# Two gate tiles of each merge step computed from seven block products instead of eight in chunks 1 to 3

## The reference

```python
h = rmsnorm(x, norm_g)
proj = h @ w_in                     # 1024 x 9216; the last 3072 columns are the gates
y_a = (conv module, width 31) @ w_a_out
y_b = (differential attention, 4 heads) @ w_b_out
y_c = (short gated convolution, width 3) @ w_c_out
g = sigmoid(gates + gate_b).reshape(b, s, 3, 1024)
merged = g[:, :, 0] * y_a + g[:, :, 1] * y_b + g[:, :, 2] * y_c
out = rmsnorm(x + merged @ w_o, final_g)
```

## Time and profile before

| | |
|---|---|
| median of 3 runs | 2287.43 us (2286.47 to 2288.08) |
| the profiled execution | 2287.08 us, its span 2285.3 us |
| TensorE busy | 2258.3 us, 99% of the span |
| VectorE, ScalarE, GpSimd busy | 62%, 33%, 10% |
| granted TensorE clock | 0.999 of the full 2.4 GHz |
| the three merge stages of chunks 1 to 3 | 133.6, 133.6 and 134.0 us |
| DMA | 493.53 MB, mean 216 GB/s |

### The profile page before, as it was taken

One profiled execution on the slowest core, in us unless ns is written; L12 is line 12 of the kernel. 1 busy time (PEld: TensorE's weight loads), 2 busy tenths in 40 slices (PEclk: granted clock), 3 DMA queues, 4 the chain that ended last, 5 costly groups with the idle time before them and its releaser, 6 DMA issues.

```text
span 2285.3 us, 29046 instructions
## 1 busy us (share of the span) xinstructions
PE 2258.3 (99%) x10822; PEld 1833.4 (80%) x10822; DVE 1425.9 (62%) x2706; ACT 756.3 (33%) x1610; POOL 232.9 (10%) x186
## 2 busy tenths in 40 slices
PE   7999999999999999999999999999999999999998
PEld 6888888878888888888788788888877787788886
DVE  4767667774666675554566667665546656677752
ACT  4334332342333331021344344102135445441121
POOL 3544400100000000010000000001000000000010
PEclk9999999999999999999999999999999999999999
DMA  8877788788566665566655565556775555545555
GB/s 312 287 267 265 269 289 290 273 326 325 163 202 196 180 153 193 200 241 249 258 182 173 171 195 159 169 187 239 262 260 143 174 163 168 158 135 184 187 192 201
DMA packets 99339, 493.53 MB, mean 216 GB/s; under 512 B 15360, under 2 KB 18304, under 8 KB 54144
## 3 DMA queue, kind: packets, MB, share of 16 engines
q1 hardware_dynamic: 90464, 488.90, 63.9%
q10 hardware_dynamic: 8736, 2.78, 0.6%
HBM read 378.37 MB, written 113.27 MB: 215 GB/s over the span
## 4 chain that ended last, share of the span: by engine, by line
PE 95%; DVE 2%; DMA 1%; issue 1%; ACT 1%; SPq 0%; DVEq 0%; ACTq 0%
PE PJ L768 74%; PE SC L827 6%; PE SC L859 5%; PE TB L868 3%; PE OB L892 1%; PE OB L893 1%; PE OB L827 1%; PE PJ L827 1%; PE OB L895 1%; PE OB L894 1%; PE TB L903 0%; DMA PX<-x_t 0%; DMA UC<-x 0%; PE TB L919 0%; DVE Wp L1341 0%
## 5 line engine op out<-in xcount | busy, mean ns | idle before, releaser
L768 PE MATMUL PJ<-hT,Wp 128*128 128x512 f32 x6480 | 1571.6, 394 | 0.5 <-DVE PX L1631 0.5
L768 PEld LDWEIGHTS PJ<-hT,Wp 128*128 128x128 f32 x6480 | 1189.5, 188 | 254.2 <-issue 17.7
L1551 DVE SCALAR_TENSOR_TENSOR ACCS<-UA,col,ACCS 128x512 f32<-128x512 f32 x464 | 350.7, 798 | 0.4
L1065 ACT ACTIVATE PX<-SC,negm 128x512 f32<-128x512 f32 (+3 forms) x320 | 196.2, 623 | 145.7 <-DVE negm L1380 143.8
L1425 DVE TENSOR_TENSOR ZA<-TB,ZA 128x512 fp32r<-128x512 f32 (+1 forms) x144 | 95.1, 661 | 176.9 <-ACT ZA L1085 176.0
L1380 DVE TENSOR_REDUCE negm<-SC 128x2 f32<-128x1024 f32 (+3 forms) x160 | 169.0, 1062 | 40.2 <-PE SC L859 37.6
L1085 ACT ACTIVATE ZA<-TB 128x512 fp32r<-128x512 f32 (+1 forms) x144 | 82.7, 574 | 322.1 <-PE TB L868 322.1
L1136 ACT ACTIVATE TG<-PJ,col 128x512 f32<-128x512 f32 x64 | 44.1, 689 | 348.1 <-PE PJ L768 348.0
L1418 DVE SCALAR_TENSOR_TENSOR PX<-PX,sc 128x512 f32<-128x512 f32 (+3 forms) x160 | 108.1, 696 | 51.0 <-ACT PX L1076 50.8
L827 PE MATMUL SC<-Wp,KM 128*128 128x512 f32 x384 | 121.4, 389 | 0.0
L1076 ACT ACTIVATE PX<-PX,sc 128x512 f32<-128x512 f32 (+3 forms) x160 | 98.9, 655 | 64.9 <-DVE sc L1407 44.6
(11 more groups left out here) (192 smaller groups left out, 2038.5 us busy)
## 6 DMA issues: line engine op xcount, KB each, us to landing
Wp<-split_weights SPq DMA_DIRECT2D x264, 1024.0 KB, 4.8
split_weights<-Wp SPq DMA_DIRECT2D x88, 1024.0 KB, 4.9
Wraw<-w_stream SPq DMA_DIRECT2D x88, 512.0 KB, 5.9
KM<-keys SPq DMA_DIRECT2D x24, 512.0 KB, 5.9
VM<-values SPq DMA_DIRECT2D x24, 512.0 KB, 6.4
PX<-x SPq DMA_DIRECT2D x16, 512.0 KB, 7.8
out<-PX SPq DMA_DIRECT2D x16, 512.0 KB, 10.6
keys<-KM SPq DMA_DIRECT2D x12, 512.0 KB, 9.6
```

The source lines that it names most:

```text
L768: mm = pe.matmul(pj(c, r)[:, :], wt, rhs[:, 1 if q == 1 else 0, k, :], start=(n == 0), stop=(n == 3 * ktiles - 1))
L1065: a = act.activation(probs(c, h, t, j, m)[:, 0:w], SC[k][:, m, 0:w], ACT.Exp, bias=negm[:, t % 2, j, m:m + 1], accum_out=lsum[:, t % 2, j, ...
L1551: a = dve.scalar_tensor_tensor(out=acc, in0=src, scalar=col[:, n:n + 1], in1=acc, op0=ALU.mult, op1=ALU.add)
```

## The change

In chunks 1 to 3 the two gate tiles of a merge tile, a 256 x 1024 by 1024 x 512 product, are treated as 2x2 blocks: weight blocks of 128 rows by 512 (4 K-tiles), inputs in halves of K and of the 512 columns (`HALF` = 256). Seven block products take the place of eight (Winograd's form), each 12 matmuls of 256 columns: 84 short matmuls instead of 48 of 512 columns.

- Three products (A11, A12, A22) use weight blocks of the stream itself: they are loaded raw again (256 KB each) and split anew by ScalarE and GpSimd. Four (S1 to S4) use sums of weight blocks: these are formed once, in chunk 1's head stage, by VectorE (32 operations), split by ScalarE and GpSimd (32 each) and stored to HBM (`wsum`), then loaded per merge tile in all three chunks (512 KB each).
- The matching sums of the input's blocks (`turned_sums`) are formed by VectorE from step 508 of the chunk before, split by ScalarE and VectorE, stored (`tz`) and loaded back into `KM` and `VM` (`TS`, `TU`) when the chunk's attention has finished with them: 2 MB each.
- The seven results go to quarter banks of `SC`. ScalarE copies A11 to `P1` and A12 to `TG`, GpSimd adds the two (the first quarter), VectorE does six more additions of 128x256 (`add_quarter`); `gate` then works in place on `TG`.
- `Wp` becomes 6 half slots. The 16 gate tiles of the merge stage are no longer stored in chunk 0 (16 MB less written).
- Lists of times shift: more taps in the head stage (`HEAD_TAPS` 58, 46, 24, 0 becomes 58, 72, 78, 50), `LN_AT` 408, 408, 408, 414 becomes 400, 408, 408, 408, the input chain (`XN_AT`) 4 steps later in chunks 1 and 2, 8 in chunk 0.

```diff
-W_SLOTS = 3
+SLOTS = 6
+HALF = CHUNK // 2
+A11, S1, S2, A12, S3, S4, A22, YB, YC = range(9)
+SUM_ORDER = (S1, S3, S2, S4)
-OSUM_LAG = (10, 10, 10, 9)
+OSUM_LAG = (10, 11, 10, 9)
-DIRECT_SPREAD = (19, 15, 15, 15)
+DIRECT_SPREAD = (19, 15, 15, 17)
-LN_AT = (408, 408, 408, 414)
+LN_AT = (400, 408, 408, 408)
-LN_SPREAD_AT = 13
+LN_SPREAD_AT = 15
-XN_AT = 444
-XS_AT = 460
+XN_AT = (452, 448, 448, 0)
+XS_AT = (468, 460, 460, 0)
+RAW_AT = ((0, 0, -14), (0, 1, -13), (1, 1, -9))
+SPLIT_AT = ((A11, -6), (A12, -5), (A22, 0))
+QUARTER_AT = (6, 7, 10, 10, 12, 12)
+SECOND_AT = 7
+BLOCK_AT = ((S1, -9), (S2, -7), (S3, -3), (S4, 0), (YB, 4), (YC, 6))
+SUM_AT = 24
+SUM_STEP = 8
+SUMS_AT = 508
+SUMS_STORE_AT = (20, 40)
+X_LOAD_AT = (442, 444)
+SUMS_BACK_AT = 272
-HEAD_TAPS = (58, 46, 24, 0)
+HEAD_TAPS = (58, 72, 78, 50)
-AFTER_FROM = 268
+AFTER_FROM = 272
...
+            def gates_part(c, m, part):
+                n0 = merge_at(c, m)
+                for n in range(PRODUCTS * part, PRODUCTS * (part + 1)):
+                    b, i = divmod(n, 3 * KB)
+                    k, q = divmod(i, 3)
+                    if i == 0:
+                        weight_ready(c, mid_block(m, b))
+                        if b == A11:
+                            wait(pe, quarter_done, QUARTERS * (n0 - 1) + 3)
+                            if m == 0:
+                                for s in range(2):
+                                    pe.wait_ge(sc_free[s], units_before(c + 1) // 2)
+                        elif b == S1:
+                            wait(pe, quarter_done, QUARTERS * (n0 - 1) + 4)
+                            if m == 0:
+                                pe.wait_ge(t_back[0], 64 * c)
+                        elif b == S2:
+                            wait(pe, quarter_done, QUARTERS * (n0 - 1) + 5)
+                        elif b == A12:
+                            wait(pe, quarter_done, QUARTERS * n0)
+                        elif b == S3:
+                            pe.wait_ge(p1_copied, n0 + 1)
+                            if m == 0:
+                                pe.wait_ge(t_back[1], 64 * c)
+                        elif b == S4:
+                            pe.wait_ge(quarter_done, QUARTERS * n0 + 1)
+                        elif b == A22:
+                            pe.wait_ge(p2_copied, n0 + 1)
+                    l = 1 if q == 1 else 0
+                    rows = {A11: hT[:, l, k, 0:HALF], S1: TS[:, l, k, 0:HALF], S2: TS[:, l, k, HALF:],
+                            A12: hT[:, l, KB + k, 0:HALF], S3: TU[:, l, k, HALF:], S4: hT[:, l, KB + k, HALF:],
+                            A22: TU[:, l, k, 0:HALF]}[b]
+                    mm = pe.matmul(P_BANKS[b], Wp[:, block_slot(c, mid_block(m, b)), 1 if q == 2 else 0, k * P:(k + 1) * P], rows,
+                                   start=(i == 0), stop=(i == 3 * KB - 1))
...
+            def weight_sum(m, k):
...
+                dve.tensor_tensor(dst, x0, x1, op).then_inc(sum_ready, 1)
+            def add_quarter(c, m, k):
+                n = merge_at(c, m)
+                b, src, dst, after = ((S2, P1[:, :], C22, 0), (S1, C22, C12, 1), (S3, C22, C21, 1),
+                                      (S1, C21, C22, 3), (S4, C12, C12, 2), (A22, C21, C21, 3))[k]
...
+                dve.tensor_tensor(dst, P_BANKS[b], src, ALU.add).then_inc(quarter_done, 1)
+            def sum_high(m, k):
+                act.wait_ge(sum_ready, 4 * m + k + 1)
+                wait(act, sum_stored, 16 * (4 * m + k))
...
+            def copy_first(c, m):
...
+                act.activation(P1[:, :], P_BANKS[A11], ACT.Copy).then_inc(p1_copied, 1)
+            def copy_second(c, m):
...
+                act.activation(C11, P_BANKS[A12], ACT.Copy).then_inc(p2_copied, 1)
+            def block_lo(c, m, b):
...
+                pool.tensor_tensor(Wp[:, s, 1, :], raw_home(c, *raw_of(m, b)), Wp[:, s, 0, :].bitcast(F32),
+                                   ALU.subtract).then_inc(w_lo, 1)
+            def add_first(c, m):
+                pool.wait_ge(p2_copied, merge_at(c, m) + 1)
+                pool.tensor_tensor(C11, C11, P1[:, :], ALU.add).then_inc(c11_done, 1)
+            def load_sums(c, k):
+                if k == 0:
+                    sp.wait_ge(qk_done, units_before(c + 1))
+                else:
+                    sp.wait_ge(pv_done, turns_before(c + 1))
...
```

More of the change, by code:

```diff
@@ new lines, in merge_tile, with gate_tile, block_before, count_tables @@
+def merge_tile(i):
+    return W_MID <= i < W_YA
+def gate_tile(i):
+    return merge_tile(i) and (i - W_MID) % 3 < 2
+def block_before(c, q):
+    n = block_at(c, q) - SLOTS
+    if n < B_FIRST:
+        return 0, n
+    c, q = divmod(n - B_FIRST, B_CHUNK)
+    return c + 1, q
+def count_tables():
+    low, stored, back = {}, {}, {}
+    stores, backs, n = [0] * SLOTS, [0] * SLOTS, 0
+    for i in range(W_CHUNK):
+        n += 1
+        low[0, 2 * i] = low[0, 2 * i + 1] = n
+        if not gate_tile(i):
+            s = block_slot(0, 2 * i)
+            stores[s] += 1
+            stored[i] = (s, stores[s])
+    for c in range(1, NCHUNK):
+        units = [(2 * i, 2) for i in range(W_MID)]
+        units += [(mid_block(m, k), 1) for m in range(M_OUT) for k in range(MID_BLOCKS)]
+        units += [(tile_block(c, i), 2) for i in range(W_YA, W_CHUNK)]
+        for q, size in units:
+            if B_MID <= q < B_YA and (q - B_MID) % MID_BLOCKS in (A11, A12, A22):
+                n += 1
+                low[c, q] = n
+            else:
+                s = block_slot(c, q)
+                backs[s] += 1
+                for k in range(size):
+                    back[c, q + k] = (s, backs[s])
+    return low, stored, back
@@ L109, in units_before @@
+RAW, RAW_ORDER = raw_table()
+SUM_ORDER = (S1, S3, S2, S4)
 def units_before(c):
@@ L338, in room_table @@
 def room_table(c):
-    free = [(r, None) for r in range(SPARE if c == 0 else 4 * KB)]
+    free = [(r, None) for r in range(SPARE[c] if c < 2 else 4 * KB)]
     room, last = {}, {}
@@ L603, in build @@
+        C11, C12, C21, C22 = [TG[:, i, j * HALF:(j + 1) * HALF] for i in range(2) for j in range(2)]
         block = ctx.enter_context(nc.Block())
@@ L711, in _ @@
+                    if c > 0 and p == SUMS_BACK_AT:
+                        load_sums(c, 0)
+                    if c > 0 and p == max(TURNED[c]) + PV_LAG[c] + 1:
+                        load_sums(c, 1)
+                    for k in range(2):
+                        if c > 0 and p == SUMS_STORE_AT[k]:
+                            store_sums(c, k)
                     if c > 0 and p == 0:
```

543 lines of the change are left out of this document (425 added, 118 removed).

## The result

The changed kernel takes 2296.96 us (median of 6 runs, 2294.61 to 2304.51), the kernel before in the same sitting 2287.47 (6 runs): ratio 1.0049, 95% interval 1.0039 to 1.0059. It is slower by 0.5%, where the prediction said 2263.5, faster by 1%, with 2252 to 2277 as its range. The profiled execution took 2297.87 us, its span 2296.1, so the traces are to explain 10.8 us.

What follows compares the result with a forecast made beforehand. TensorE's sum of matmuls was taken to bound the kernel (busy 2258.3 of 2285.3 us). Terms: -27.3 + 2 (`TU`) + 1 (head) + 0.6 (layer norms) = -23.7, giving 2263.5 us, range 2252 to 2277.

Steps and rivals of the forecast that it cites:

- the signs that were to show it wrong: Short matmuls settling above 120 ns, or chunk 1's head stage growing by more than 3 us.
- The gate matmuls: Merge tiles: 84 short matmuls at 116 ns replace 48 long ones, 1.14 us less a tile, -27.3 us.
- Columns alone: Rival: columns alone pace the short gate matmuls, 113.3 ns each, giving 2257 us; chance 0.20.
- Waits inside a tile: Merge tiles: copies and additions feeding the products are covered by other matmuls; cost 0, 12 us without cover.
- DMA, the step that failed: Merge stages and chunk 1's head: block loads covered at 259 and 280 GB/s; only loading `TU` costs, 2 us.
- VectorE: Chunk 1's head: VectorE at 77%, at most 82% with slowed taps; 1 us there, 0.2 us each layer norm.
- The side engines take the gain back: Rival: VectorE held by GpSimd and `sum_high` waiting for stores, chunk 1's head and merge tiles; +15 us, 2278, chance 0.13.
- Late `TU`: Rival: first merge tile's S3 waits for the `TU` load, 4 us in each chunk; +10, 2273, chance 0.05.
- Input sums and input chain: Chunk starts: input additions and splits fit VectorE's idle time, scales still 1.4 us early; cost 0 each.

Runs made afterwards that it cites:

- e11_before8: Kernel before, only its stores of output scales packed as 128 packets of 8 bytes instead of 256 of 4; 2287.25 us, ratio 1.0001.
- e7_order_ts: Changed kernel with two rooms for the sums, YC ahead in the queue, later `TS` load (chunk 1) and raw halves (chunks 2, 3); 2274.59 us, ratio 0.9946.
- e3_taps46: Changed kernel with the taps in chunk 1's head stage back from 72 to 46; 2303.03 us, ratio 1.0076.
- e10: e7_order_ts with the stores of output scales packed as 128 packets of 8 bytes; 2269.64 us, ratio 0.9925.
- e2_two_rooms: Changed kernel with a second room for the weight sums, so a split waits for the store before the last; 2289.93 us, ratio 1.0012.
- e6_no_sums: Changed kernel with YC ahead in the queue and the forming of the 32 weight sums left out; 2275.35 us.
- e12_after8: Changed kernel, only its stores of output scales packed as 128 packets of 8 bytes; 2282.45 us, ratio 0.9982.

## Why the prediction was wrong

It had the sign wrong. The forecast was -23.7 us, the profiled executions differ by +10.8. Of these 34.5 us about 8.5 are the pace of the short matmuls, 15 the late weight blocks of the merge stages and 15 chunk 1's way to its merge stage; 3.5 came back in chunk 0. Of the signs that were to show it wrong, chunk 1's head stage came true (+12.6 us, the limit was 3), and the short matmuls settled just at the other limit, 120 ns.

- **The gate matmuls.** Right in kind, mis-sized: 120 ns a matmul where I took 116, -18.8 us instead of -27.3. The value was the bound that I had written down from the second gap of each pair. That second gap was the sustained pace; the first followed a long matmul. The rival *Columns alone* falls with it. This term costs 8.5 us.
- **Waits inside a tile.** Right: no gap in any undisturbed tile.
- **DMA, the step that failed.** "A block is issued 8 or more steps ahead and 1024 KB land in 4.8 us. Covered." Three things were wrong in it. First, I took the volume for the test (280 GB/s asked, 278 shown) and not the moments: behind the stores of scales the queue nearly halts for 4 to 10 us, and an average of a stage doesn't show it. The 278 came from chunk 0's heads, where no scales are stored (the first store is at 619 us). With the queue busy 0.63 of the time the halts cost nothing (packing the stores brought nothing, e11_before8), with 0.89 they did: the sum's store landed late, and ScalarE, VectorE and TensorE waited behind it in turn. Removing the stores from the changed kernel gives 14 us, packing them 14.5. Second, I did not write out the order of the queue at the end of the merge stage: YC stands behind `x` and a tile of branch a. With the order changed the merge stages give 6.0, 6.3 and 4.3 us, with the edits of e7_order_ts 5.9, 6.0 and 5.7. Third, "8 or more steps ahead" was not so for that block: it was issued 5.1 us ahead of its use and took 8 us, where the median I had counted on was 4.8 for 1024 KB.
- **VectorE.** I put 1 us on chunk 1's head, for VectorE's load. Its load cost nothing (e3_taps46), and the mean tap takes 819 ns as before, where I had 0.22 us more for every tap of the head: 5 of 66 were held, the others not. The head took 12.6 us more, for the queue.
- **The rival *The side engines take the gain back*** named half of the mechanism, ScalarE's `sum_high` behind the store of the sum before, and gave it +15 us. It reckoned with 5 us of landing, by which the wait would have been covered, and so with 0.3 us a sum; what happened was 15 waits of 5 us in the mean and 8.4 at most, of which TensorE felt a few. That its +15 lies near chunk 1's 16.0 is luck: a third of it was to come from the merge tiles, which lost nothing to the side engines. Its result, 2278, was counted from a gain of 27 that was 19, and the measured time lies outside its range too.
- **Late `TU`** was not seen: S3 never waits for a DMA. The first merge tile of chunk 3 lost 2.8 us, 1.8 of them a wait for its YC, of a kind with the last tiles.
- **The clock** was in no term. The wait of 3.1 us was followed by 6.8 us at the 1.2 GHz level, which costs about as much again as the wait.
- **Input sums and input chain.** 0.5 us in the rest of chunk 1, 1.2 in chunk 2's first head: small, as said. Not in the sum at all: chunk 0's merge stage is 3.4 us shorter, 134.6 instead of 138.0, with the queue at 172 GB/s there where it was at 292. That the 16 MB less written are the cause is argued, not tried.

What the change is worth with the queue in order is e10: 2269.64, 17.3 us less than before, or by stages -17.9 in the three merge stages, -3.4 in chunk 0's, and +2.5 in branch a of chunks 1 and 2, which was moved later in the queue.

## What to carry to other kernels

Before a change that fills a DMA queue, look at the queue in windows of 2 us, not of a stage: here a queue that halted 21 times was harmless while it was busy 0.63 of the time, and cost 14 us at 0.89. Write out the order of the queue ahead of each wait of TensorE, for a transfer is late behind one that nobody needs yet, and behind the wait for that one's slot. Where an instruction was only seen in pairs, the second gap was the sustained pace here and the mean was not. And a mean over many instructions can stay the same although some of them are held for more than their own time.

## What the runs showed of the hardware that was not expected

- Stores of 256 packets of 4 bytes, 1 KB in all, were followed by a slow stretch of 4 to 10 us: in the one shown the DMA engines moved 20 to 99 GB/s instead of 385, and packets of 8192 bytes, which mostly take 0.31 us, took 1.5 to 8.1. The stores are ScalarE's and the slow packets those of SyncE's queue. As 128 packets of 8 bytes the stretch is about half as long, and slow packets fall from 479 to 236 (changed kernel) and from 524 to 211 (before). Whether the number of packets or their size does it is open, since both changed together. The Trainium skill, DMA: Bandwidth & Descriptors, section "Rules for kernel authors", says of many small transfers to coalesce them for their own overhead; the cost here fell on the other transfers.
- The pace of matmuls with a weight load each, at the 2.4 GHz level: 111 ns at 128 columns, 120 at 256, 173.6 at 384, 226.7 at 512.
- TensorE's waits of 3.1 and 2.8 us (changed kernel, last merge tiles), 3.3 (e2_two_rooms) and 3.9 us (e6_no_sums) were each followed by 3.4 or 6.8 us at the 1.2 GHz level. Shorter ones went either way: the waits of up to 2.1 us in chunk 1's heads of the changed kernel were not, those of 2.1 and 1.9 us in the merge stages of e12_after8 were, by 3.4 us each.
- A tap of VectorE (0.74 us) that started while a GpSimd instruction was running ended 0.55 us after it and took up to 1.8 us in chunk 1's heads.
